# Up projection of a convolutional decoder step: seven block products by Strassen's identity in place of eight

## What is computed

```python
h2 = _rmsnorm(x, g_ffn)
f = jnp.einsum("btd,df->btf", h2, w_up)          # 1024 -> 2 x 2816
f_gate, f_up = jnp.split(f, [D_FF], axis=-1)
f_conv, new_f = _causal_dwconv(f_gate, buf_f, conv_f_w)   # 3 taps
x = x + jnp.einsum("btf,fd->btd", jax.nn.silu(f_conv) * f_up, w_down)
...
y = _rmsnorm(x, g_final)
```

## Time and profile before

| | us |
|---|---|
| median of 3 runs (lowest, highest) | 868.17 (867.98, 868.20) |
| profiled execution, its own time | 867.93 |
| its span in the profile | 866.0 |
| PE busy (share of the span) | 857.0 (99%) |
| DVE busy | 608.9 (70%) |
| ACT busy | 350.5 (40%) |
| POOL busy | 115.7 (13%) |

### The profile page before, as it was taken

The page is one execution under the profiler, slowest core; times in us unless marked ns, Lnnn a source line. Parts: engine busy times, 40 slices in busy tenths (PEclk is TensorE's granted clock), DMA queues, the critical chain, the costliest instruction groups (busy, mean ns, idle before and its releaser), DMA issues.

```text
span 866.0 us, 19056 instructions
## 1 busy us (share of the span) xinstructions
PE 857.0 (99%) x7116; PEld 854.0 (99%) x7116; DVE 608.9 (70%) x923; ACT 350.5 (40%) x588; POOL 115.7 (13%) x82
## 2 busy tenths in 40 slices
PE   8999999999999999999999999999999999999997
PEld 7999999999999999999999999999999999999996
DVE  5899999999999956664677766666666666234334
ACT  8654636464342335652234533332233323332232
POOL 2383837384000000000000000000000000000000
PEclk9999999999999999999999999999999999999999
DMA  8433242533333332319633242332333322344433
GB/s 255 131 90 98 75 117 77 158 97 86 106 98 97 98 108 75 98 38 162 169 94 97 68 129 81 88 96 78 93 97 97 97 67 71 103 121 107 92 80 111
DMA packets 189142, 88.66 MB, mean 102 GB/s; under 512 B 34759, under 2 KB 187645, under 8 KB 189077
## 3 DMA queue, kind: packets, MB, share of 16 engines
q1 hardware_dynamic: 186225, 86.29, 37.0%
q10 hardware_dynamic: 2875, 1.82, 0.7%
HBM read 83.79 MB, written 3.51 MB: 101 GB/s over the span
## 4 chain that ended last, share of the span: by engine, by line
PE 98%; ACT 1%; DVE 0%; ACTq 0%; issue 0%; DVEq 0%
PE psum L1223 62%; PE psum L1229 31%; PE psum L1426 1%; PE psum L1434 1%; PE psum L1267 1%; PE psum L1274 0%; PE psum L1265 0%; PE psum L1201 0%; PE psum L1334 0%; PE psum L1312 0%; ACT act L453 0%; ACT L429 0%; DVE y L1160 0%; ACT w_hi L444 0%; ACT tmp L435 0%; PE psum L1195 0%
## 5 line engine op out<-in xcount | busy, mean ns | idle before, releaser
L1223 PE MATMUL psum<-act,w_hi 128*128 128x260 f32 x2600 | 340.8, 282 | 0.0
L1223 PEld LDWEIGHTS psum<-act,w_hi 128*128 128x128 f32 x2600 | 322.8, 188 | 0.0
L1223 PE MATMUL psum<-mid,w_hi 128*128 128x260 f32 x1920 | 249.3, 282 | 0.0
L777 DVE TENSOR_TENSOR w_lo<-raw,w_hi 128x1024 fp32r<-128x1024 f32 (+2 forms) x154 | 185.1, 1202 | 88.8 <-ACT w_hi L408 87.8
L1223 PEld LDWEIGHTS psum<-mid,w_hi 128*128 128x128 f32 x1920 | 238.1, 188 | 0.0
L408 ACT ACTIVATE w_hi<-raw 128x1024 fp32r<-128x1024 f32 (+2 forms) x154 | 155.0, 1007 | 193.6 <-PE psum L1229 188.7
L1229 PE MATMUL psum<-act,w_lo 128*128 128x260 f32 x1300 | 185.2, 282 | 0.0
L1229 PEld LDWEIGHTS psum<-act,w_lo 128*128 128x128 f32 x1300 | 168.2, 188 | 0.0
L1229 PE MATMUL psum<-mid,w_lo 128*128 128x260 f32 x960 | 135.1, 283 | 0.0
L1229 PEld LDWEIGHTS psum<-mid,w_lo 128*128 128x128 f32 x960 | 123.4, 188 | 0.0
L393 POOL TENSOR_TENSOR gate_a<-gate_a,prods 128x512 f32<-128x512 f32 x72 | 110.0, 1527 | 79.7 <-ACT prods L493 71.3
(11 more groups left out here) (162 smaller groups left out, 483.6 us busy)
## 6 DMA issues: line engine op xcount, KB each, us to landing
raw<-in_w_in SPq DMA_DIRECT2D x56, 512.0 KB, 3.9
raw<-in_w_up SPq DMA_DIRECT2D x44, 512.0 KB, 3.8
raw<-in_w_down SPq DMA_DIRECT2D x16, 384.0 KB, 3.4
raw<-in_w_down SPq DMA_DIRECT2D x16, 320.0 KB, 3.0
v<-in_x_prompt SPq DMA_DIRECT2D x8, 512.0 KB, 7.1
raw<-in_w_b_out SPq DMA_DIRECT2D x8, 512.0 KB, 3.8
raw<-in_w_a_out SPq DMA_DIRECT2D x8, 512.0 KB, 5.8
raw<-in_w_o SPq DMA_DIRECT2D x8, 512.0 KB, 4.1
```

Source lines behind the costliest of these rows:

```text
L777: ve.tensor_tensor(w_lo[:, s, 0:k, :], raw[:, s, 0:k, :], w_hi[:, s, 0:k, :], ALU.subtract).then_inc(lo_done, 1)
L1223: pe.matmul(a[:, h, :], w_hi[:, s, j, :], rhs[:, 2 * k + part, h * H:(h + 1) * H], start=start and part == 0, stop=False)
```

## The change

The 1024 inputs are taken as two halves (even tiles and odd tiles), the 520 columns as two halves of 260, and the two outputs of a pair (gate, up) as two block rows. The pair is then a 2x2 by 2x2 block product, and Strassen's identity in its form with 15 additions (Winograd's) computes it with seven block products, P1 to P7, instead of eight. Each product is 4 input tiles x 3 passes = 12 matmuls of 128x260. The identity needs, for each pair, four sums of weight blocks (128x512 each), four sums of token blocks (made once, as `T1` to `T4`, and kept with `B11`, `B21` and `B22` in high and low parts), and sums of the products.

- **GpSimd** makes the sums of token blocks (`token_sum`, 16 of 128x260) while the `w_o` projection runs, and for every pair the sums of weight blocks S1, S2, S3 (`weight_sums`) and S4 (`weight_sum_4`). It also multiplies the SiLU with `rinv` (`gain`, 128x520), so that the up tile needs no `rinv` of its own.
- **ScalarE and VectorE** split four weight sets a pair: 1 (raw gate row, 128x1024), 2 (S1 and S2, 128x1024), 3 (128x1024) and 4 (one block, 128x512): 3584 columns in place of 2048.
- **ScalarE** copies P1, P1 + P6 and P5 out of PSUM (`snap_1`, `snap_v`, `snap_5`, 128x260 each), and VectorE adds them to other banks (`up_11`, `up_22`, `up_12`), half a tile at a time. Products that share an addend accumulate in the same PSUM bank, so TensorE waits for the copies in between.
- The first convolution tap moves to ScalarE (`conv_first`); the taps on the 8 sample columns are partly prepared ahead (`side_state`).
- Product tiles lie in `act` as raw values first; high parts and low parts of tiles 0 to 9 are made in the loop, those of 10 to 21 after it (`up_hi`, `up_lo`).
- One SyncE loop loads both rows of a pair when the pair before the last has been split.
- The turn of the state rows (`turn_tail_f`) goes behind the first output tile of the down projection.

The steps of the new loop, cut to their core:

```diff
+            def weight_sums(n, par, first=False):
+                gate, up = 2 * par, 2 * par + 1
+                pool.wait_ge(raw_in[gate], raw_up(n, par))
+                pool.wait_ge(raw_in[up], raw_up(n, par))
...
+                    pool.wait_ge(q_lo, group(n - 1, G2))
+                pool.tensor_tensor(s1_s2[:, 0], raw_even(up), raw_odd(up), ALU.add).then_inc(w_sum, 1)
+                pool.wait_ge(w_sum, RING * n + 1)
+                pool.tensor_tensor(s1_s2[:, 1], s1_s2[:, 0], raw_even(gate), ALU.subtract).then_inc(w_sum, 1)
+                pool.tensor_tensor(raw_even(up), raw_even(gate), raw_even(up), ALU.subtract).then_inc(w_sum, 1)
+            def weight_sum_4(n, par):
+                pool.wait_ge(w_sum, RING * n + 2)
+                pool.wait_ge(q_lo, group(n, G1))
+                pool.tensor_tensor(raw_odd(2 * par), raw_odd(2 * par), s1_s2[:, 1], ALU.subtract).then_inc(w_sum, 1)
+            def gain(i):
+                pool.wait_ge(silu_done, START + i + 1)
+                pool.wait_ge(rinv_done, 2)
+                pool.tensor_tensor(t1, t1, rinv, ALU.mult).then_inc(gain_set, 1)
...
+                    weight_sums(n + 1, 1 - odd)
+                    gain(n - 1)
+                    weight_sum_4(n + 1, 1 - odd)
...
+            def up_step(n, par, split, last=False):
+                hi_4(n, par)
+                up_1(n, par)
+                conv_first(n - 1)
+                hi_3(n, par)
+                silu(n - 1)
...
+                    hi_1(n + 1, 1 - par)
+                up_v(n, par)
+                up_5(n, par)
+                if split:
+                    up_hi(n - 1)
...
+                    hi_2(n + 1, 1 - par)
...
+            def up_12(i, par):
+                ve.wait_ge(p_done, p1_of(i) + P3)
+                ve.wait_ge(snap, 3 * i + 2)
+                ve.tensor_tensor(cx[:, PADB + H:PADB + N], bank_y(par), snap_v, ALU.add).then_inc(c12_set, 1)
...
+                ve.tensor_tensor(cx[:, PADB:PADB + N], cx[:, PADB:PADB + N], rinv, ALU.mult).then_inc(cx_set, 1)
+            def up_product(i, par, p=None):
+                ve.wait_ge(gain_set, i + 1)
+                ve.wait_ge(p_done, p1_of(i + 1) + P4_BEFORE if p is None else p)
+                ve.tensor_tensor(act_f(i)[:, 0:H], bank_x(par), t1[:, 0:H], ALU.mult).then_inc(x_read, 1)
+                ve.wait_ge(c22_set, i + 1)
+                ve.tensor_tensor(act_f(i)[:, H:N], c22, t1[:, H:N], ALU.mult).then_inc(prod_done, 1)
...
+            def up_step(n, par, split, last=False):
+                up_12(n - 1, 1 - par)
+                lo_2(n)
+                conv_rest(n - 1)
+                lo_4(n, par)
+                lo_3(n, par)
...
+                    lo_1(n + 1, 1 - par)
+                up_product(n - 1, 1 - par)
+                up_11(n, par)
+                up_22(n, par)
+                if split:
+                    up_lo(n - 1)
...
+            def up_step(n, par, first=False):
...
+                product("P1", n, par)
+                pe.wait_ge(c22_set, n)
+                product("P4", n - 1, 1 - par, first=first)
...
+                product("P2", n, par)
+                pe.wait_ge(snap, 3 * n + 1)
+                product("P6", n, par)
...
+                product("P5", n, par)
+                pe.wait_ge(snap, 3 * n + 2)
+                product("P7", n, par)
+                pe.wait_ge(snap, 3 * n + 3)
+                product("P3", n, par)
```

More of the change, by code:

```diff
@@ L664, in _ @@
+            up_1(0, 0, first=True)
+            hi_3(0, 0, first=True)
+            hi_1(1, 1)
+            up_v(0, 0, first=True)
+            up_5(0, 0, first=True)
+            hi_2(1, 1)
             sc.wait_ge(var_eps, 2)
@@ new lines, in _ @@
+            for first, end, split in ((0, EARLY_HI // 2, True), (EARLY_HI // 2, FT // 2 - 1, False)):
+                with sc.Fori(first, end) as it:
+                    for odd in (1, 0):
+                        up_step(2 * it + 2 - odd, odd, split)
+            up_step(FT - 1, 1, False, last=True)
+            for i in range(EARLY_HI, EARLY_HI + 3):
+                up_hi(i)
+            down_hi(2, p1_of(FT - 1) + P3)
+            conv_first(FT - 1)
+            for i in range(EARLY_HI + 3, EARLY_HI + 5):
+                up_hi(i)
@@ new lines, in down_lo @@
+            def down_lo(s):
+                lo_split(G_DOWN + s, s, KSPLIT[s], slot=DOWN_SLOT[s])
+            lo_2(0)
+            sum_lo_split(2, ssum)
+            lo_4(0, 0)
+            lo_3(0, 0)
+            lo_1(1, 1)
+            root_eps(2, square_banks, RMS_EPS)
+            up_11(0, 0, first=True)
+            up_22(0, 0, first=True)
+            root_inverse(2)
+            def up_step(n, par, split, last=False):
[4 more added lines that the diff above has]
+                lo_3(n, par)
+                if last:
+                    down_lo(0)
+                else:
+                    lo_1(n + 1, 1 - par)
[4 more added lines that the diff above has]
+                    up_lo(n - 1)
@@ new lines, in _ @@
+            for first, end, split in ((0, EARLY_HI // 2, True), (EARLY_HI // 2, FT // 2 - 1, False)):
+                with ve.Fori(first, end) as it:
+                    for odd in (1, 0):
+                        up_step(2 * it + 2 - odd, odd, split)
+            up_step(FT - 1, 1, False, last=True)
+            up_12(FT - 1, 1)
+            down_lo(1)
+            conv_rest(FT - 1)
+            down_lo(2)
+            for i in range(EARLY_HI, EARLY_HI + 3):
+                up_lo(i)
+            down_lo(3)
@@ L1311, in mean_over_features @@
                     for h in range(2):
[L1312 removed]
+                        last = pe.matmul(psum[:, banks + h, 0:H], ones_r, SUM_SPLIT[n][part][:, h * H:(h + 1) * H],
                                          start=part == 0, stop=part == 1)
@@ L1433, in _ @@
                     for j in range(KSPLIT[s]):
-                        last = pe.matmul(last_acc(part), w_lo[:, s, j, :], act[:, 2 * (KFIRST[s] + j), lo:hi], start=False,
+                        last = pe.matmul(last_acc(part), w_lo[:, DOWN_SLOT[s], j, :], in_down(KFIRST[s] + j, 0)[:, lo:hi], start=False,
                                          stop=s == RING - 1 and j == KSPLIT[s] - 1)
```

527 lines of the change are left out of this document (387 added, 140 removed).

## The result

The changed kernel takes **921.37 us** (median of 4 runs, 921.08 to 922.27), the kernel before 868.08 (867.94 to 868.20) beside it: a ratio of 1.0616, 95% interval 1.0597 to 1.0634. It is slower by 53.3 us. The forecast was 926.5, with a range of 885 to 950 and 0.9 on slower. The profiled execution took 921.39 us, its span 919.6.

A forecast was written before the change was run, and what follows sets the result against it. TensorE bounded the kernel before; afterwards VectorE and GpSimd taking turns on SBUF would. Step 1 at 497, ten steps of 14.5 and ten of 13.8 give 780; down at 790, span 924.5, plus 1.95: 926.5 us, range 885 to 950.

The forecast's parts named there:

- VectorE's own list, 8.4 and 9.0: Up projection loop: VectorE's own work takes 8.4 us a step, 9.0 with up_lo, under TensorE's 10.07.
- GpSimd 6.5 alone, and the exclusion: Loop: GpSimd needs 6.5 us a pair; its instructions and VectorE's that read or write only SBUF run in turn.
- The late step, 13.8: Loop steps without up_lo, ten of them: laid out from the start of up_12 on VectorE, 13.8 us each.
- The early step, 14.5: Ten loop steps with up_lo: 14.4 us, plus 0.1 for ScalarE's chain to the first tap, 14.5 each.
- The last step, 10, and the end: Step 21, without sums, takes 10 us; down begins at 790, then 134.0 to the end and 0.4 for moved transposes.
- The head, 497: Before the loop: up_1 near 486, lo_3 near 490, then square root and 3.40 reciprocal; step 1 starts near 497.
- Transfers, nothing: Weight loads: 1 MB a pair, issued together at lo_3, wanted 7 us later; nothing was put for them.
- Markers: Signs in the profile after: GpSimd sums over 1.9 us, TensorE idle 25 to 30%, first ten steps longer by 0.7.
- packed: Loop: GpSimd's instructions find VectorE's PSUM work and waits as their time, 885 to 908 us; chance 0.2.
- lost turns: Loop: ScalarE's queue or a lost race costs VectorE one more 1.3 us sum a step, 940 to 955; chance 0.15.
- No exclusion: Loop: sums and remainders overlap and TensorE bounds, 842 us, up to 855 with an odd wait; chance 0.08.
- clock: Loop: TensorE, idling in holes of 1 to 3 us, falls to 1.2 GHz, 1015 us; chance 0.04.

The follow-up runs named there:

- the placed version: Changed kernel with only S1 and S4 left on GpSimd, S2, S3 and gain on VectorE, taps in PSUM, product halves exchanged, up_hi and up_lo later: 857.09 us.
- the short one: Changed kernel with the reciprocal ahead of step 1 on 8 columns in place of 520: 918.94 us.

## Why the prediction was right, point by point

The sign, the cause and the size were right, though one term, the early step, was right by luck. The 5.1 us between 926.5 and 921.4 come from terms as follows: head +0.8, early steps -1.1, late steps -5.1, last step +0.5, time around the span -0.2.

- **TensorE, 264 matmuls less.** Right, and where TensorE bounds they are real: the placed version has them in its 10.3 us a step. In the changed kernel they buy nothing.
- **VectorE's own list, 8.4 and 9.0.** Borne out by the version with all sums on VectorE: 8.4 + 5 x 0.61 = 11.5 and 12.1, measured 11.8 and 12.4. The 0.3 between them was missing in each. In that trace VectorE sits idle some 0.24 us a step ahead of S1, which needs the `lo_2` just before it, and as long ahead of the product, which needs the gain just before it: dependences between neighbours that the sum of durations leaves out.
- **GpSimd 6.5 alone, and the exclusion.** Right: S4 1.28 where nothing meets it; all other meetings at 1.6 to 2.3. With half the columns a sum takes 0.735 in place of 1.28. "Reads or writes only SBUF" should have been "has both data inputs in SBUF, or has its one data input and its result there", as far as these runs show.
- **The late step, 13.8.** Measured 13.29, the mis-sized term: 10 x 0.5 = 5 us, nearly all of the difference. Counted from the add (L1396, 0.45 ahead of L1399 at 708.61), `lo_2` ends at 2.2 in place of 2.4, since a multiply behind a 260-column add starts 0.45 after it, not 0.6; S3 ends at 7.6 in place of 8.0, because the 8 columns and `lo_4` slip in at the change of hands; `lo_3` 8.65 in place of 9.1. From there to the end the layout runs 0.4 to 0.5 behind the trace without more loss.
- **The early step, 14.5.** Measured 14.39 in the mean, but not by the way laid out. It is 1.1 longer than a late one, where `up_lo` and 0.1 for ScalarE's chain gave 0.7. The second tap hardly waited for ScalarE's first (0.3 us in the whole loop, at L1408). VectorE waited instead for `up_hi` ahead of `up_lo` (L1043, 3.4 us over ten steps, 0.34 each), which the sum does not have. Had the late step not been 0.5 too long, this would have missed by 0.4: two errors cancel, which is luck.
- **The last step, 10, and the end.** From the add at 774.62 to the first matmul of the down projection at 785.17 it took 10.55, and from there to the end 134.4, as laid out. The last `lo_3` had GpSimd out of its way and lasted 1.22.
- **The head, 497.** The step's first add is at 497.80; `up_1` starts at 485.10 and `lo_3` ends at 490.5, where 486 and 490 stood. The reciprocal lies at 494.05 to 497.45 on VectorE, in the path, as the short one showed.
- **Transfers, nothing.** Right in the changed kernel: no wait for DMA is among its larger ones. In the placed version S1 does wait for a transfer, 32.2 us in total, at no cost that the late step shown has: S1 ends at 641.98 there, and VectorE comes to S2, which needs it, at 642.63.
- **Markers.** Three failed. TensorE was to be idle 25 to 30%; it shows 20% in the early half and 16% in the late one. The matmuls of the late half say otherwise (897 x 0.12 = 107.6 us of 140, 23% idle): a short run of matmuls is busy longer than its number times the distance, because the last one's whole duration counts, so busy time understates waits once the work is cut in pieces. "Sums over 1.9" was high: 1.3 to 1.8, with only the gain at 2.26. And the first ten steps are longer by 1.1, not by 0.7.

The larger waits of TensorE and GpSimd (waiting tile, releaser, us in total, times, longest) agree with "waiting on VectorE" only at one remove:

```profile
POOL w_sums L491 <- DVE w_lo L1338: 79.5, 20, 6.0
ACT tmp L897 <- DVE tmp L1410: 60.1, 21, 4.1
...
PE psum L1770 <- ACT tmp L879: 44.3, 20, 3.8
```

TensorE waits for ScalarE, but ScalarE's `snap_v` (L879) stands in its list behind the SiLU (L897), and that waited for VectorE's held 8 columns (L1410). A releaser is the last link of a chain, and the cause lay two links behind it.

Of the **rivals**, packed and lost turns would each have moved the steps by over 1 us from 13.8 and 14.5, and no mean did by more than 0.5. No exclusion is excluded by the experiments. The **clock** rival is half right. These are matmuls of the head, three runs of six of the same size:

```profile
485.52 1.20 PE L1770 MATMUL psum<-act,w_hi 128*128 128x260 f32 x6 [3.21 <-ACT u L873]
...
487.81 1.50 PE L1770 MATMUL psum<-mid,w_hi 128*128 128x260 f32 x6
...
490.03 0.88 PE L1770 MATMUL psum<-mid,w_hi 128*128 128x260 f32 x6
```

After a wait of 3.21 us six matmuls take 1.20 and then 1.50 us, and soon afterwards 0.88 again. The granted clock is 1.00 up to 486.0, half a microsecond into the matmuls, then 0.50 up to 489.5: the lower level, 1.2 GHz, for some 3.4 us. In the loop the granted clock has a mean of 0.89 from 500 to 640, down to 0.70 in one stretch of 10 us, and 0.98 from 640 to 780, where it was 1.00 throughout before. The waits of the early steps are the longer ones (for L879, 1.5 to 3.8 us, against 1.4 to 2.4 in the late steps), but the length of one wait does not tell whether the clock falls: the matmuls behind one of 2.34 us (520.05) ran at the lower level, and behind one of 2.64 us (606.68) the clock stayed at 1.00. The Trainium skill, page "TensorE: Matmul & The Clock Gate", section "HAM oscillation", says that a kernel with repeated waits falls again and again; its example waits longer than most of the waits here. It did here, but the price was small: the step with the 0.70 is 14.70 us long, its neighbours 14.4 and 14.5. That the time is hidden where TensorE would wait for VectorE in any case fits this, but no run had the same waits without the fall. With 0.04 I had priced the whole rival, fall and cost together; the fall was likely, and only its cost was not.

## What to carry to other kernels

Before elementwise work goes to an idle GpSimd, look at what VectorE does in that time: beside instructions with two SBUF inputs, or a multiply by a factor from SBUF to SBUF, it is not a second engine but a slower turn on the first (1.28 us for what costs VectorE 0.61), while beside instructions that take an input from PSUM it is free (additions of 260 columns stay at 0.42 and wide taps at 0.755 there, as with GpSimd idle). So count one shared list per step, place GpSimd's pieces beside read-outs of PSUM, and give VectorE back the rest; here that, with the edits beside it, turned 53 us lost into 11 won. And held time costs only where the engine that is held is the bound.

## What the hardware showed that I had not expected

- An instruction on 8 columns with two SBUF inputs is held for the whole of a GpSimd instruction of 512 columns, 1.19 to 1.26 us for work of 0.22, even when it writes to PSUM. Narrow helpers are the dearest to place beside GpSimd.
- A TENSOR_SCALAR with one data input, SBUF to SBUF, is held as well: 1.31 us in place of 0.49 for 512 columns, 1.00 in place of 0.23 for 8.
- A wait of 3.21 us was followed, 0.5 us after the matmuls had begun again, by some 3.4 us at 1.2 GHz. In a stage that waits for another engine such falls cost little: at most 0.4 us in the step with the lowest clock.
- 24 us in 100 of added holding on VectorE left the kernel's time unchanged within 0.1%.
